# mLSTM heads of a two-layer mixer: spreads ahead of values, both directions weighed ahead of finishing, and the addition of the directions folded into a multiplication

## The reference, cut to what matters

```
b = jnp.cumsum(fc, axis=-1)
d = jnp.where(causal, b[..., :, None] - b[..., None, :] + ic[..., None, :], -jnp.inf)
m_t = jnp.maximum(inter, jnp.max(d, axis=-1))
s = jnp.einsum('bhtd,bhsd->bhts', qc, kc) * jnp.exp(d - m_t[..., None])
num = jnp.einsum('bhts,bhsv->bhtv', s, vc) + ...
den = jnp.sum(s, axis=-1) + ...
h = num / jnp.maximum(jnp.abs(den), jnp.exp(-m_t))[..., None]
...
return hc_f + _flip_t(hc_b), hl_f + _flip_t(hl_b)
```

## Time and profile before

| | |
|---|---|
| median of 3 runs | 1890.7 us |
| lowest, highest | 1890.65, 1893.2 us |
| the profiled execution, first to last instruction (span) | 1892.8 us |
| stage of the mLSTM heads in it | 198.8 to 281.3 us |

### The profile page before, as it was taken

One profiled execution on the slowest core, in us unless ns is written; L12 is line 12 of the kernel. 1 busy time (PEld: TensorE's weight loads), 2 busy tenths in 40 slices (PEclk: granted clock), 3 DMA queues, 4 the chain that ended last, 5 costly groups with the idle time before them and its releaser, 6 DMA issues. The chain is left out here.

```text
span 1892.8 us, 23753 instructions
## 1 busy us (share of the span) xinstructions
PE 1775.1 (94%) x8820; PEld 1468.7 (78%) x8820; DVE 1372.5 (73%) x1457; ACT 1032.5 (55%) x1250; POOL 132.3 (7%) x139
## 2 busy tenths in 40 slices
PE   8999779899999997999988869999999999999997
PEld 2788667787787876887877658888888888888886
DVE  4685578654554565776459559898989898989898
ACT  3643554522222225423344448787878787878775
POOL 2351120000000000000003020000000000000002
PEclk9999999899999998999998969999999999999999
DMA  9353263443433552444310439999999999999996
GB/s 319 132 177 112 76 222 106 159 143 135 139 128 134 166 189 89 135 148 151 134 46 1 167 112 383 347 406 350 407 352 406 347 406 347 408 349 408 355 407 220
DMA packets 148808, 436.23 MB, mean 230 GB/s; under 512 B 8394, under 2 KB 31090, under 8 KB 148605
## 3 DMA queue, kind: packets, MB, share of 16 engines
q1 hardware_dynamic: 146232, 430.92, 62.0%
q0 software_dynamic: 1152, 4.19, 0.6%
q10 hardware_dynamic: 1350, 0.11, 0.1%
HBM read 416.59 MB, written 16.25 MB: 229 GB/s over the span
## 5 line engine op out<-in xcount | busy, mean ns | idle before, releaser
L2925 DVE TENSOR_TENSOR w_low<-e_ring,w_high 128x1536 fp32r<-128x1536 f32 x383 | 611.5, 1621 | 85.3 <-ACT w_high L2829 84.1
L2829 ACT ACTIVATE w_high<-e_ring 128x1536 fp32r<-128x1536 f32 (+1 forms) x381 | 520.1, 1380 | 158.5 <-PE ps L2747 135.8
L2745 PE MATMUL ps<-w_high,list_h 128*128 128x512 f32 (+1 forms) x768 | 290.9, 379 | 4.4 <-DVE list_l L2943 4.2
L2747 PE MATMUL ps<-w_high,list_l 128*128 128x512 f32 (+1 forms) x768 | 287.0, 374 | 0.0
L2746 PE MATMUL ps<-w_low,list_h 128*128 128x512 f32 (+1 forms) x768 | 286.9, 374 | 0.0
L1806 ACT ACTIVATE fw_high<-ring 128x1024 fp32r<-128x1024 f32 x62 | 65.7, 1060 | 262.7 <-PE ps L1735 190.7
L1857 DVE TENSOR_TENSOR fw_low<-ring,fw_high 128x1024 fp32r<-128x1024 f32 x62 | 76.0, 1225 | 150.2 <-ACT fw_high L1806 150.2
L2745 PEld LDWEIGHTS ps<-w_high,list_h 128*128 128x128 f32 x768 | 144.9, 189 | 26.3 <-issue 4.6
L2747 PEld LDWEIGHTS ps<-w_high,list_l 128*128 128x128 f32 x768 | 144.7, 188 | 21.1
L2746 PEld LDWEIGHTS ps<-w_low,list_h 128*128 128x128 f32 x768 | 145.0, 189 | 20.6
L1733 PE MATMUL ps<-u_high,fw_high 128*128 128x512 f32 x352 | 141.2, 401 | 7.6 <-DVE fw_low L1857 7.6
(11 more groups left out here) (450 smaller groups left out, 3326.8 us busy)
## 6 DMA issues: line engine op xcount, KB each, us to landing
e_ring<-in_e_w_gu_dram SPq DMA_DIRECT2D x96, 1536.0 KB, 8.9
e_ring<-in_e_w_down_dram SPq DMA_DIRECT2D x48, 1536.0 KB, 8.7
bg_area<-in_mod_w_dram SPq DMA_DIRECT2D x72, 512.0 KB, 4.1
e_ring<-in_e_w_gu_dram SPq DMA_DIRECT2D x32, 1024.0 KB, 7.7
ring<-in_f_w_gu_dram SPq DMA_DIRECT2D x22, 1024.0 KB, 7.8
ring<-in_h_w_in_dram SPq DMA_DIRECT2D x10, 2048.0 KB, 8.0
e_ring<-in_e_w_down_dram SPq DMA_DIRECT2D x16, 1024.0 KB, 6.6
ring<-in_m_w_in_dram SPq DMA_DIRECT2D x6, 2048.0 KB, 8.7
```

Source lines behind the costliest of these rows:

```text
L2745: nc.tensor.matmul(out, high[:, f, :], w_high[:, c, :], start=(f == 0), stop=False)
L2747: last = nc.tensor.matmul(out, low[:, f, :], w_high[:, c, :], start=False, stop=(f == total - 1))
L2829: nc.scalar.activation(piece(k.w_high, p), raw_piece(k, p), ACT.Copy).then_inc(S.high_done, 1)
L2925: nc.vector.tensor_tensor(piece(k.w_low, p), raw_piece(k, p), piece(k.w_high, p).bitcast(F32), ALU.subtract).then_inc(S.low_done, 1)
```

## The change

- TensorE: for each head h the order becomes spread(2h+2), values(2h), scores(h+1), spread(2h+3), values(2h+1). Backward values take the tiles in the order 2, 3, 0, 1, and tile 0 waits for the finishing of the turn before, with tile 1 behind it. The backward tiles are placed one step closer, tile 1 now in bank 6.
- VectorE: for each head weigh(2h), weigh(2h+1), finish(2h-1), perhaps low halves, finish(2h), perhaps low halves.
- Finishing of a forward turn multiplies into one of two buffers, by the head's parity. Finishing of a backward turn is four instructions of 128x128, each value times reciprocal denominator plus the forward part, into `tok`. GpSimd's additions and their semaphore are gone.
- ScalarE: the high halves of pair 1's queries come ahead of the first exponential; the others, and the low halves, move to other turns. Squares of head h come behind the exponentials of turn 2h + 4 and wait for VectorE.

```diff
--- before.py
+++ after.py
@@ -1144,14 +1144,14 @@
     nc = k.nc
     scored, spread, weighed, probs = k.sem("a_scored"), k.sem("a_spread"), k.sem("a_weighed"), k.sem("a_probs")
     m_cleared = k.sem("a_m_cleared")
-    masked, summed, own, added = k.sem("a_masked"), k.sem("a_summed"), k.sem("a_chain"), k.sem("a_added")
+    masked, summed, own = k.sem("a_masked"), k.sem("a_summed"), k.sem("a_chain")
     turn_done, squares, rooted, m_split = k.sem("a_turn_done"), k.sem("a_squares"), k.sem("a_rooted"), k.sem("a_m_split")
     prob = k.u_area.rearrange("p (b s t) -> p b s t", b=2, s=NT)
     decay = k.ex[:, 0:4 * HALF].rearrange("p (s t) -> p s t", s=NT)
-    part = k.ex[:, 4 * HALF:6 * HALF].rearrange("p (b t) -> p b t", b=2)
+    forward = lambda h: k.ex[:, (4 + h % 2) * HALF:(5 + h % 2) * HALF].rearrange("p (i c) -> p i c", i=NT)
     turns = 2 * HEADS
 
-    V_STEP, V_FIRST = 171, (5 * HALF, 6 * HALF + 345)
+    V_STEP, V_FIRST = 171, (5 * HALF, 5 * HALF + 4 * 171)
     flat_ps = k.ps.rearrange("p b n -> p (b n)")
 
     def value_of(d, i):
@@ -1167,8 +1167,8 @@
 
     split_q, split_k, low_q, low_k = k.sem("a_split_q"), k.sem("a_split_k"), k.sem("a_low_q"), k.sem("a_low_k")
     twice_in = [k.sem(f"a_twice_in{n}") for n in range(2)]
-    HIGH_IN = {0: (1, "q"), 1: (1, "k"), 3: (2, "q"), 4: (2, "k"), 7: (3, "q"), 8: (3, "k")}
-    LOW_IN = {1: (1, "q"), 2: (1, "k"), 4: (2, "q"), 5: (2, "k"), 8: (3, "q"), 9: (3, "k")}
+    HIGH_IN = {0: (1, "k"), 2: (2, "q"), 4: (2, "k"), 6: (3, "q"), 8: (3, "k")}
+    LOW_IN = {(0, 0): (1, "q"), (0, 1): (1, "k"), (1, 1): (2, "q"), (2, 0): (2, "k"), (3, 1): (3, "q"), (4, 0): (3, "k")}
     PAIRS = HEADS // 2
     own_rows, other_rows = (slice(0, M_DK), slice(M_DK, P)), (slice(M_DK, P), slice(0, M_DK))
     stacks = lambda pair, kind, odd: k.stacks[(pair - 1) % 2][kind][odd]
@@ -1243,7 +1243,7 @@
                 pe.wait_ge(masked, n + 1)
                 if n >= 2:
                     pe.wait_ge(summed, n - 1)
-                for i in (0, 1, 2, 3) if d == 0 else (1, 2, 3, 0):
+                for i in (0, 1, 2, 3) if d == 0 else (2, 3, 0, 1):
                     js = SOURCES[d][i]
                     if n and i == (3 if d == 0 else 0):
                         pe.wait_ge(summed, n)
@@ -1256,20 +1256,21 @@
             scores(0)
             spread_m(0)
             spread_m(1)
-            for n in range(turns):
-                if n % 2 == 0 and n:
-                    scores(n // 2)
-                    spread_m(n)
-                    spread_m(n + 1)
-                if n:
-                    values(n - 1)
-            values(turns - 1)
+            for h in range(HEADS):
+                last_head = h == HEADS - 1
+                if not last_head:
+                    spread_m(2 * h + 2)
+                values(2 * h)
+                if not last_head:
+                    scores(h + 1)
+                    spread_m(2 * h + 3)
+                values(2 * h + 1)
 
         @block.scalar
         def _(act):
             def squares_of(h):
 
-                act.wait_ge(added, h + 1)
+                act.wait_ge(summed, 2 * h + 2)
                 if h >= 2:
                     act.wait_ge(squares, NT * (h - 1))
                 for i in range(NT):
@@ -1295,10 +1296,9 @@
             for d, src in enumerate((k.scan_m, k.scan_m_rev)):
                 act.wait_ge(m_split, 2 * d + 2)
                 nc.scalar.activation(k.m_both[0:16, d, :], src[0:16, :], ACT.Copy).then_inc(m_split, 1)
+            high(1, "q")
             for n in range(turns):
                 h, d = n // 2, n % 2
-                if n >= 5 and n % 2:
-                    squares_of((n - 5) // 2)
                 act.wait_ge(spread, n + 1)
                 for j in range(NT):
                     t0, t1 = (x * P for x in SEEN[d][j])
@@ -1308,6 +1308,8 @@
                                          bias=k.a_cols[:, j, 8 * d + h:8 * d + h + 1]).then_inc(weighed, 1)
                 if n in HIGH_IN:
                     high(*HIGH_IN[n])
+                if n >= 4 and n % 2 == 0:
+                    squares_of((n - 4) // 2)
             squares_of(HEADS - 2)
             act.wait_ge(squares, NT * (HEADS - 1))
             sums = head_sums(k, 0, HEADS - 1)
@@ -1343,10 +1345,15 @@
                 chain.link(nc.vector.scalar_tensor_tensor(out=den, in0=out_den, scalar=-1.0, in1=den,
                                                           op0=ALU.mult, op1=ALU.max))
                 chain.link(nc.vector.reciprocal(den, den))
-                if n >= 2:
-                    dve.wait_ge(added, n // 2)
-                nc.vector.tensor_tensor(part[:, d, :].rearrange("p (i c) -> p i c", i=NT), out_values,
-                                        den.unsqueeze(2).to_broadcast([P, NT, DV]), ALU.mult).then_inc(summed, 1)
+                if d == 0:
+                    nc.vector.tensor_tensor(forward(h), out_values, den.unsqueeze(2).to_broadcast([P, NT, DV]),
+                                            ALU.mult).then_inc(summed, 1)
+                    return
+                dve.wait_ge(summed, n)
+                for i in range(NT):
+                    last = nc.vector.scalar_tensor_tensor(out=k.tok[:, i, h * DV:(h + 1) * DV], in0=value_of(d, i)[:, 0:DV],
+                                                          scalar=den[:, i:i + 1], in1=forward(h)[:, i, :], op0=ALU.mult, op1=ALU.add)
+                last.then_inc(summed, 1)
 
             def low(pair, what):
                 for odd in range(2):
@@ -1360,12 +1367,16 @@
                         nc.vector.tensor_tensor(k.k_low[rows, :], k.qk[rows, 4 + pair, :],
                                                 words(pair, "k", odd)[rows, :], ALU.subtract).then_inc(low_k, 1)
 
-            for n in range(turns):
-                weigh(n)
-                if n:
-                    finish(n - 1)
-                if n in LOW_IN:
-                    low(*LOW_IN[n])
+            for h in range(HEADS):
+                weigh(2 * h)
+                weigh(2 * h + 1)
+                if h:
+                    finish(2 * h - 1)
+                if (h, 0) in LOW_IN:
+                    low(*LOW_IN[h, 0])
+                finish(2 * h)
+                if (h, 1) in LOW_IN:
+                    low(*LOW_IN[h, 1])
             finish(turns - 1)
             dve.wait_ge(rooted, 1)
             sums = head_sums(k, 0, HEADS - 1)
@@ -1374,13 +1385,6 @@
 
         @block.gpsimd
         def _(pool):
-            def add(h):
-
-                pool.wait_ge(summed, 2 * h + 2)
-                hv = k.tok[:, :, h * DV:(h + 1) * DV]
-                pool.tensor_tensor(hv, part[:, 0, :].rearrange("p (i c) -> p i c", i=NT),
-                                   part[:, 1, :].rearrange("p (i c) -> p i c", i=NT), ALU.add).then_inc(added, 1)
-
             pool.memset(k.m_both[0:32, :, :].bitcast(F32), 0.0).then_inc(m_cleared, 1)
             pool.memset(k.zero_rows, 0.0).then_inc(zeros_made, 1)
             for n in range(turns):
@@ -1392,9 +1396,6 @@
                 sign = 1 if d == 0 else -1
                 pool.affine_select(out=diag, in_=diag, compare_op=ALU.is_ge, fill=0.0, base=0,
                                    pattern=[[0, NT], [sign, P]], channel_multiplier=-sign).then_inc(masked, 1)
-                if d == 1 and n > 1:
-                    add(n // 2 - 1)
-            add(HEADS - 1)
 
 
 
```

## The result

The changed kernel takes 1899.3 us (median of 10 runs, 1893.5 to 1904.1), the kernel before 1893.5 in the 10 runs beside it: ratio 1.0029, with an interval of 1.0017 to 1.0041. By the ratio that is 5.5 us slower. A second batch gave 1.0040 (1.0026 to 1.0053). The forecast was 1.5 us more and no change; the measured time lies above the range. The median of the kernel before also stood at 1893.2 over 35 runs, so that the three runs shown first (1890.7) were low by 2.5 us; the ratio is free of that, and it is what has to be explained. On a base of 1893.5 the forecast of 1.5 us more would have been 1895.0.

The account below looks back on a forecast made before the run. The prediction took a head's spread loop of 7.88 us, tied with GpSimd's wait, as the bound; new loops of 8.86 to 9.41 put the scaling at 279.8 for 278.26, +1.5 on 1890.7: 1892.2 us, range 1888.5 to 1896.0.

Parts of the forecast that it names:

- The loop: Plain mLSTM head, scores to scores through second weighing, finishing 2h-1 and the even values' last tile: 8.86 us, before 7.88.
- last tile: TensorE's last of four tiles of even values, 4 of 10 matmuls, waits for finishing 2h-1 and takes 0.90 us.
- The loops with splits: Heads that also split the next pairs into high and low halves: loops of 9.00, 9.41 and 9.00 us.
- the sum: Heads stage laid end to end: scores of head 7 at 266.2, scaling at 279.8 for 278.26 before, +1.5 us.
- The multiply-add: One 128x128 piece of VectorE's odd-turn finishing takes about 0.34 us, occupies 0.26 with overlap; four take 1.04.
- The rival in which the pieces don't overlap: VectorE's odd-turn finishing: each multiply-add costs its full 0.34 us, stage 4.1 us longer, 1894.8 us; chance 0.05.
- The rival of GpSimd's waits: VectorE's 10.0 us of waits for GpSimd's addition were the path, so the kernel gets faster, 1885.4 us; chance 0.06.
- The end of the stage: From the scores of head 7 to the last scaling: 13.6 us, with the scaling starting at 279.8.
- the clock: Rival: TensorE's clock falls after waits of 2.2 to 2.7 us in even values; two such heads give 1897.0; chance 0.03.
- the first stretch: Stage start to second scores: from 210.49 to 211.8, as two high halves put 1.30 us before the first exponential.
- What the stage loses passes on whole: Heads stage is closed at both ends, so its gain or loss, here +1.5 us, reaches the kernel's time whole.

Follow-up runs that it names:

- Experiments 5: The changed kernel with finishing 2h-1 put between the two weighings of a head: ratio 0.9975, heads stage 77.7 us.
- 6: The changed kernel with the even values' last tile waiting only for the two multiply-adds that read its bank: ratio 0.9998, heads stage 80.5 us.
- experiment 4: The kernel before, in its old order, with GpSimd's addition folded into four multiply-adds: ratio 1.0012, heads stage 83.7 us.
- experiments 3: The changed kernel's new order with the old finishing and GpSimd's addition: ratio 1.0004, heads stage 82.8 us.
- experiment 8: The kernel before with three spent VectorE maxima ahead of the last scaling, as a plain delay: ratio 1.0013, heads stage 86.2 us.
- 7: The changed kernel with six matmuls repeated while TensorE waits for the even values' fourth tile: ratio 1.0010, 1895.3 us, heads stage 84.3 us.

## Why the prediction was wrong

- *The loop, as forecast.* All terms but one were right within 0.02 us: scores to spread 1.55 (257.46 less 255.89 is 1.57), odd values 2.50, second weighing 1.73 (1.74), finishing 0.59 + 1.13 with the last piece's tail (forecast 1.64 and 0.14 for tail and signal), last tile 0.92. A spread alone takes 0.43; the forecast had 0.32, from two in a row. In sum 9.02 for 8.86. The loops with splits, forecast at 9.00, 9.41 and 9.00, took 9.01, 9.40 and 9.00. The scores of head 7 start 67.7 us into the stage where the sum had 67.4. Experiments 5 and 6 show that this loop sets the time.
- *The multiply-add, as forecast.* One takes 0.344 us, and four take 1.13 to the last end: three starts of 0.26 and one whole length. The rival in which the pieces don't overlap falls. The prediction gave only half of what the Trainium skill, "VectorE: DVE Perf Modes", says in section "The DRAIN you can't avoid": the next operation does not start until the pipe is empty, but one that is not held starts earlier. The trace shows the second case, each piece starting 0.08 before the end of the one ahead. The counsel of fewer operations is not in that section.
- *The rival of GpSimd's waits* fell in experiment 4.
- *The end of the stage* was off both ways. The scaling takes 2.29 us in place of 3.04, with no addition of GpSimd beside it (2.29 in experiment 4 too, 3.22 in 3, and 2.29 in 8, which is the kernel before with the addition over by then): a gain of 0.75 that I had priced at nothing. The addition in the trace of before, from the timeline of GpSimd:

```profile
277.89 1.26 POOL L1381 TENSOR_TENSOR tok<-ex 128x512 f32<-128x512 f32 x1 [2.97 <-DVE ex L1348]
```

  The Trainium skill, "GPSIMD Engine Reference", section "8. Key points", says that GpSimd shares its SBUF interfaces with VectorE and contends with instructions that have two SBUF inputs; the scaling has two, and the traces agree. Against the gain, the last turn took 1.55 us more on the lower clock.
- *The step that failed is the clock.* I gave its fall a chance of 0.03 and no term in the sum, with the argument that the old stage had waits of up to 2.8 us at a full clock. No such wait stands there: the 2.8 in the table of waits is two of 1.4 together, and behind the first values the longest single wait is 2.23. Waits of TensorE, and the row of the longest, in the trace of before:

```profile
PE ps L1214 <- DVE u_area L1332: 2.8, 2, 1.4
...
221.40 0.47 PE L1214 MATMUL ps<-stack_q_high,stack_k 128*128 128x512 f32 x1 [2.23 <-DMA stack_k<-k_low]
```

  The changed kernel waits in each of seven heads, 1.1 to 2.3 us. In all eight traces of it, with the halves early or back, the clock fell behind the last of them (2.26 or 2.27 us), and in three also behind the one of 2.02. It held in experiments 3 and 6, whose waits at that place are 1.83 and 1.75, and in 7, where all but 0.92 us of the wait is filled with matmuls. But it also held after 2.23 in the kernel before and after 2.67 in experiment 4, so the length of one wait does not decide it by itself. That the seven waits act together is my reading and is not shown. I also took the first stretch as before, though 1.3 us came ahead of the first exponential and one lone spread came into TensorE's wait. The clock cost 1.55 us at the end in all five traces of the changed kernel, and 6.1 us more in two of them (4.6 at the start, 1.5 behind the wait of 2.02). The mean of the heads stage is 88.1 us for 83.0: 5.1 us, where my sum had 1.5. The clock makes 4.0 of the 5.1 (1.55, and two fifths of 6.1); the other 1.1 are the 1.5 of the sum, 0.35 of loops that it had too short, less the 0.75 of the scaling.
- *"What the stage loses passes on whole"* failed too. The projection behind it is 1.1 us shorter than before, and the opening of HGRN2 is at 224.0 in all eight traces of the changed kernel, with the halves early or back, against a mean of 221.0 before: 3.0 us more. 5.1 - 1.1 + 3.0 = 7.0, and the mean times are 7.3 apart in the second batch (1900.2 less 1892.9), but 5.4 in the first. The mean of before comes from four traces that spread from 218.0 to 224.6. The longer opening does not go along with the order of the heads: experiments 3, 6 and 7 have that order, and 219.8, 219.6 and 219.4 us. The eight traces have in common the fall of the clock at the end of the heads stage, which these three lack; before, without that fall, still had 224.6 once. The granted clock of the opening is 0.96 where it takes 224 us and 0.99 where it takes 218. What carries it there over 400 us of the feed-forward was not found. The delay of experiment 8 had it at 218.2, so in that trace a stage 3.4 us longer did not do it.
- *The range* was built from the instruction's price and the spread of three runs. The price was good. The three runs were not: they spread over 2.5 us and lay 2.5 to 2.8 below later medians, where ten runs went from 1890.7 to 1897.1. From a base of 1893.5 the forecast is 1895.0 and still 4.3 us short of 1899.3; what was missing was a term for the clock at either end of the stage and behind it.

## What to carry to other kernels

Before putting a weighing, or any long step, ahead of a finishing step, ask which engine's next wait ends on that finishing, and what stands behind the waiting instruction; here it was 4 of 10 matmuls and all of the next head's scores, and moving the finishing back by one step turned 0.3% slower into 0.25% faster. A stage whose TensorE waits often should be priced twice, at a full clock and with one more fall of the clock, even where single waits of the same length were harmless. In a table of waits, read the longest and not the total. One trace isn't enough for that: the first trace of the changed kernel was its third fastest run of ten, and the long form showed only in the third.

## What the runs showed of the hardware

- The same program's heads stage took 85.4 to 91.8 us in five executions with the same order of work; the rows that differ are those on the lower granted clock. Before it stayed within 0.6 us in four.
- Six spare matmuls in each wait of 1.1 to 2.3 us made the kernel 2.8 to 4.2 us faster (mean 1896.0 against 1898.8 and 1900.2).
- The granted clock held after a wait of 2.67 us in one order of work (experiment 4) and fell at one of 2.27 us in another.
- A 128x2048 multiplication of VectorE with two inputs in SBUF took 2.29 us alone, 3.04 with an addition of 128x512 on GpSimd beside it for the first 0.9 us, and 3.22 with 1.1 us of it beside.
